# A four-stage transformer step on one core: the last two weight units before each norm walked both in a row for tiles 0 to 2, instead of one tile apart

## The chip, the core and the metric

One core of a Trainium2 chip runs the whole program. The metric is the device time of one execution in microseconds (us). TensorE (PE) multiplies and transposes into PSUM, VectorE (DVE) and ScalarE (ACT) read PSUM and work in SBUF, GpSimd (POOL) works in SBUF only, SyncE (SP) issues loads. They meet through semaphores.

## What is computed

A two-layer decoder trunk over 512 prompt tokens and 64 new tokens (8 sequences of 8). Layer 0 mixes by block-sparse and dilated attention, layer 1 by gated linear attention (GLA). Each layer then has a ConvFFN, and after the mix and after the FFN stands `x <- LayerNorm(alpha*x + f(x))`:

```python
xp = layer_norm(DN_ALPHA * xp + mp, ln_mix_g[l], ln_mix_b[l])       # mp = o @ w_out
fp, cbp = conv_ffn(xp, buf0, ffn_w_up[l], ffn_conv_w[l], ffn_conv_b[l], ffn_w_down[l])
xp = layer_norm(DN_ALPHA * xp + fp, ln_ffn_g[l], ln_ffn_b[l])
```

The same is done for the 64 new tokens. So there are four norms, and in front of each a product with 1024 output columns: stage 0 is the attention output product, stage 1 the down product of layer 0, stage 2 the GLA output product, stage 3 the down product of layer 1. The result of stage 3 is the output.

## The kernel before, in words

Tokens lie in five tiles, 0 to 3 of 128 rows and tile 4 of 64 (`TILES`). Weights come in units of up to 128 x 2048 values. A unit is loaded by SP into one of two `raw` slots, split into a high part by ACT (`split_hi`, L1053) and a low part by DVE (`split_lo`, L1371), and used by PE. A product takes three matmuls per 128 rows of contraction: high by high, high by low, low by high (`three_products`, L614).

A step is one unit by one tile (`project`, L622). Its matmuls of 512 columns go into PSUM bank t for tile t, the same bank for the left and the right half of the output, and it ends with one increment of the semaphore `steps`. A unit of four contraction blocks gives a step of 12 matmuls, one of two blocks a step of 6.

- Stage 0 has two units: the first gives the left half of the output, the second the right half. A step of the second must wait until DVE has read the left half of that tile out of the same bank (`z_read`).
- Stages 1 and 3 have 12 units, six for each half. Units 10 and 11 both add to the right half; unit 11 has two blocks. Its h part, too, has to be split first: high by ACT (`h_split`, L1230), low by DVE (L1576). PE waits for it in `rows_here` (L881).
- Stage 2 has four units, two for each half; units 2 and 3 both add to the right half.

All units but the last two are walked unit by unit, tiles 0 to 4. The last two are walked in the order that the list `PAIR` (L78) gives as (which of the two units, tile). `norm_steps` (L90) puts this order together, and PE (`products_before_norm`, L802) and DVE (`residual_ln`, L1542) both walk it. `norm_sums` (L96) counts the reads of PSUM by it. `freed` (L85) tells after how many steps the first unit of the pair is done with, which is after step (0, 4).

High parts share slots by parity. So ACT can split the second unit of the pair only when the unit before the pair is done with, which is when the first step of the pair begins (stages 1 to 3). It splits the first unit of the next stage when `freed` is reached (`ln_roots`, L1151), after the square root of tile 2. POOL then makes that unit's low part (`split_after_norm`, L1892). PE waits for this low part before it turns the normalised tiles of the next stage.

For each step that completes a half of a tile, DVE adds it to x (L1523, which reads PSUM) and takes the statistics (L1525). When the right half is in, it normalises the tile: L1531, then L1536 `(x - mean) * g`, then L1538 and L1540 `* 1/sd + b`, with ACT's square root (L1155) in between. After tile 3, and before tile 4, DVE makes the low parts of the turned tiles 0 to 2 (L1381) for the next stage.

In stages 0 and 2 PE also turns the convolution's side rows, 44 transposes of 20 columns (`turn_sides`, L796), just ahead of the fifth step from the end of the pair's ten. The side rows are loaded by SP (L526). In stage 0 SP issues these loads, behind the norm's vectors (L518), only when the attention outputs of the samples are ready (`soT_ready`).

Of the kernel before, what the change touches and what calls it, by code (L numbers as in the profile page):

```python
# [74 lines left out]

PAIR = [(0, 0), (0, 1), (1, 0), (0, 2), (1, 1), (0, 3), (1, 2), (0, 4), (1, 3), (1, 4)]  # L78
NORM_UNITS = []
for k_, n_ in (("attn_out", 2), ("down0", 2 * len(DOWN_GROUPS)), ("gla_out", 4), ("down1", 2 * len(DOWN_GROUPS))):  # L80
    NORM_UNITS.append([UNIT_NO[(k_, c_)] for c_ in range(n_)])
# [3 lines left out]
def freed(n):  # L85

    return STEPS_BEFORE[n] + PAIR.index((0, NTILE - 1)) + 1 if n in PAIRED else STEPS_BEFORE[n + 1]


def norm_steps(stage):  # L90

    m = len(NORM_UNITS[stage])
    return [(c, t) for c in range(m - 2) for t in range(NTILE)] + [(m - 2 + a, t) for a, t in PAIR]

# [1943 lines left out]
```

## Time and profile before

| what | value |
|---|---|
| time, median of 3 runs | 1726.14 us (1721.52 to 1729.16) |
| the profiled execution, first to last instruction | 1727.2 us |
| PE busy | 1632.9 us (95%), clock 0.967 on average |
| DVE busy | 911.0 us (53%) |
| ACT busy | 559.0 us (32%) |
| POOL busy | 59.4 us (3%) |

The profiled execution is known by its span alone. It is 1.1 us above the median of the three timed runs and inside their spread. In the rows below, a timeline row has the start, the duration, the engine, the line, the operation, out<-in with shapes, the count, and in brackets how long the engine was idle before and who released it. A duration is the instruction's own; matmuls overlap, so the pace of a row of matmuls is read from their starts. PE idle time "<-issue" is time for which the profile shows no releaser.

### The profile page before, as it was taken

The numbers are of one execution on the slowest core, as the hardware profiler recorded it, in microseconds if no ns is written. First come the engines' busy times: TensorE is split into PE (matmuls) and PEld (weight loads), VectorE is DVE, ScalarE is ACT, GpSimd is POOL, SyncE is SP. The second block draws the span as 40 slices with busy tenths as digits, with TensorE's granted clock in tenths as the row PEclk, the third lists the DMA queues.
The fourth block names the chain that finished last, engine by engine and source line by source line (L and its number), as shares of the span: only waits on it lengthen the run. The fifth ranks groups of instructions, "written<-read, shape, count | busy, mean of one in ns | idle before, by whom it ended". The sixth has DMA issues, their size and how long they took to land.

```text
span 1727.2 us, 24786 instructions
## 1 busy us (share of the span) xinstructions
PE 1632.9 (95%) x9654; PEld 1417.9 (82%) x9654; DVE 911.0 (53%) x1718; ACT 559.0 (32%) x1040; POOL 59.4 (3%) x95
## 2 busy tenths in 40 slices
PE   6999999988899999999989999989989999999996
PEld 5888766656799999988869888866879999998885
DVE  2533243024766666653462276566566666665445
ACT  2212244331334334333222433252133433433321
POOL 1002200000100000000010000010010000000000
PEclk9999999997899999999989899999989999999998
DMA  4223550345132232242131221053113223224211
GB/s 161 95 91 101 191 220 36 109 131 127 49 98 73 73 97 73 73 119 73 62 96 51 67 73 57 25 177 113 49 53 95 73 79 91 73 73 119 74 61 55
DMA packets 150849, 155.82 MB, mean 90 GB/s; under 512 B 7598, under 2 KB 120366, under 8 KB 150542
## 3 DMA queue, kind: packets, MB, share of 16 engines
q1 hardware_dynamic: 146842, 141.70, 26.6%
q0 software_dynamic: 3936, 13.14, 2.4%
q8 instruction: 49, 0.80, 0.2%
q14 instruction: 22, 0.18, 0.0%
HBM read 142.99 MB, written 21.91 MB: 95 GB/s over the span
## 4 chain that ended last, share of the span: by engine, by line
PE 86%; DVE 8%; ACT 4%; issue 2%; DMA 0%; SPq 0%; POOL 0%; DVEq 0%; ACTq 0%; POOLq 0%
PE ps L618 70%; PE ps L599 5%; PE ps L674 2%; PE ps L781 2%; PE ps L945 1%; DVE x_reg L1536 1%; PE ps L978 1%; PE ps L1009 1%; DVE w_lo L1375 1%; ACT w_hi L1059 1%; ACT arena L1091 1%; DVE x_reg L1540 1%; DVE arena L1437 1%; DVE xl_reg L1381 1%; PE ps L708 1%
## 5 line engine op out<-in xcount | busy, mean ns | idle before, releaser
L618 PE MATMUL ps<-xh_reg,w_hi 128*128 128x288 f32 x1552 | 464.5, 299 | 7.5 <-DVE xl_reg L1381 7.5
L618 PE MATMUL ps<-xh_reg,w_lo 128*128 128x288 f32 x1552 | 460.1, 296 | 0.0
L618 PE MATMUL ps<-xl_reg,w_hi 128*128 128x288 f32 x1552 | 460.0, 296 | 0.0
L618 PE MATMUL ps<-w_hi,xh_reg 128*128 128x512 f32 x960 | 385.5, 402 | 6.9 <-DVE xl_reg L1576 3.4
L618 PE MATMUL ps<-w_lo,xh_reg 128*128 128x512 f32 x960 | 378.4, 394 | 0.0
L618 PE MATMUL ps<-w_hi,xl_reg 128*128 128x512 f32 x960 | 378.3, 394 | 0.0
L618 PEld LDWEIGHTS ps<-xh_reg,w_hi 128*128 128x128 f32 x1552 | 294.2, 190 | 9.8 <-DVE xl_reg L1381 5.4
L618 PEld LDWEIGHTS ps<-xl_reg,w_hi 128*128 128x128 f32 x1552 | 294.3, 190 | 0.0
L618 PEld LDWEIGHTS ps<-xh_reg,w_lo 128*128 128x128 f32 x1552 | 294.1, 189 | 0.0
L1375 DVE TENSOR_TENSOR w_lo<-raw,w_hi 128x2048 fp32r<-128x2048 f32 (+1 forms) x52 | 113.8, 2188 | 307.8 <-ACT w_hi L1059 307.8
L618 PEld LDWEIGHTS ps<-w_hi,xh_reg 128*128 128x128 f32 x960 | 183.3, 191 | 47.5 <-issue 7.6
L618 PEld LDWEIGHTS ps<-w_hi,xl_reg 128*128 128x128 f32 x960 | 182.9, 191 | 39.3
L618 PEld LDWEIGHTS ps<-w_lo,xh_reg 128*128 128x128 f32 x960 | 183.3, 191 | 36.2
L1059 ACT ACTIVATE w_hi<-raw 128x2048 fp32r<-128x2048 f32 (+1 forms) x55 | 100.9, 1835 | 259.6 <-PE ps L618 241.0
L1612 DVE SCALAR_TENSOR_TENSOR arena<-arena 128x512 f32<-128x512 f32 x352 | 166.8, 515 | 6.3
L1610 DVE TENSOR_SCALAR arena<-arena 128x512 f32<-128x512 f32 (+1 forms) x176 | 67.7, 427 | 179.3 <-ACT arena L1197 179.3
L1196 ACT ACTIVATE arena<-ps 128x224 f32<-128x224 f32 x88 | 31.5, 358 | 239.5 <-PE ps L618 239.5
L1594 DVE TENSOR_TENSOR w_lo<-raw,w_hi 128x2048 fp32r<-128x2048 f32 x44 | 100.5, 2285 | 3.3 <-ACT w_hi L1183 3.1
L599 PE MATMUL ps<-ident,arena 128*128 128x128 f32 (+3 forms) x434 | 65.6, 284 | 22.5 <-ACT arena L1091 6.3
L599 PEld LDWEIGHTS ps<-ident,arena 128*128 128x128 f32 (+3 forms) x434 | 47.6, 155 | 44.9 <-issue 15.3
L1183 ACT ACTIVATE w_hi<-raw 128x2048 fp32r<-128x2048 f32 x44 | 83.7, 1902 | 0.1
L1194 ACT ACTIVATE arena<-ps 128x288 f32<-128x288 f32 x88 | 36.0, 411 | 112.7 <-PE ps L618 112.7
(168 smaller groups left out, 1450.1 us busy)
## 6 DMA issues: line engine op xcount, KB each, us to landing
raw<-in_ffn_w_up SPq DMA_DIRECT2D x88, 512.0 KB, 5.0
raw<-in_ffn_w_down SPq DMA_DIRECT2D x40, 512.0 KB, 4.6
raw<-in_attn_w_in SPq DMA_DIRECT2D x24, 512.0 KB, 4.9
raw<-in_gla_w_in SPq DMA_DIRECT2D x24, 512.0 KB, 4.4
out_swa_s<-in_state_swa_kv SPq DMA_DIRECT2D x2, 3968.0 KB
x_reg<-in_x_prompt SPq DMA_DIRECT2D x8, 512.0 KB, 5.0
raw<-in_gla_w_out SPq DMA_DIRECT2D x8, 512.0 KB, 4.8
arena<-in_state_swa_kv SPq DMA_DIRECT2D x12, 256.0 KB, 3.3
```

The lines of the kernel that those rows point to most:

```text
L599: last = pe.transpose(ps[0:cols, bank, col:col + rows], src, ident[0:rows, 0:rows])
L618: mm = pe.matmul(out, lhs(i, a), rhs(i, b), start=first and i == 0 and a + b == 0, stop=last and i == ks - 1 and a == 1)
L674: pe.matmul(ps[:, g, 0:(qi + 1) * P - k0], qkT[rows, c, qi * P:(qi + 1) * P], qkT[rows, 8 + c, k0:(qi + 1) * P], start=True, stop=True).th ...
L781: pe.matmul(ps[rows, g, 0:past], qz[:, 2 * g + pair, s].rearrange("p h q -> p (h q)"), kcT[s % 2][:, b:b + past // P, :].rearrange("p b c ...
L1059: act.activation(w_hi[:, n % 2, 0:a], raw[:, n % 2, 0:a], ACT.Copy).then_inc(hi_done, 1)
L1183: act.activation(w_hi[:, slot, :], raw[:, slot, :], ACT.Copy).then_inc(hi_done, 1)
L1194: act.activation(ext[:, u, v, 2:2 + SPLIT], ps[:, m, 0:SPLIT], ACT.Copy).then_inc(ext_ready, 1)
L1196: act.activation(ext[:, u, v, 2 + SPLIT:2 + NP], ps[:, m, 0:PRE], ACT.Copy)
L1375: dve.tensor_tensor(w_lo[:, n % 2, 0:a], raw[:, n % 2, 0:a], w_hi[:, n % 2, 0:a].bitcast(F32), ALU.subtract).then_inc(lo_done, 1)
L1594: dve.tensor_tensor(w_lo[:, slot, :], raw[:, slot, :], w_hi[:, slot, :].bitcast(F32), ALU.subtract).then_inc(lo_done, 1)
L1610: ins = dve.tensor_scalar(y, e, w, fj[:, u, v, SIDE - 1:SIDE], ALU.mult, ALU.add)
L1612: ins = dve.scalar_tensor_tensor(y, e, w, y, ALU.mult, ALU.add)
```

## The change

The order of the ten steps of the pair is another. Nothing else is edited; the functions named above take the order from this list.

```diff
-PAIR = [(0, 0), (0, 1), (1, 0), (0, 2), (1, 1), (0, 3), (1, 2), (0, 4), (1, 3), (1, 4)]
+PAIR = [(0, 0), (1, 0), (0, 1), (1, 1), (0, 2), (1, 2), (0, 3), (0, 4), (1, 3), (1, 4)]
```

The second unit's steps of tiles 0, 1 and 2 are now steps 2, 4 and 6 of the ten (counted from 1), where they were 3, 5 and 7. Step (0, 4) stays the eighth, (1, 3) and (1, 4) stay the last two, so `freed` is the same number. The side rows are still turned ahead of step 6, which is (1, 2) now and was (0, 3).

## Rows read from the trace of the kernel before

**Rows 1.** The page: busy time by engine, and the chain's shares by engine.

```profile
PE 1632.9 (95%) x9654; PEld 1417.9 (82%) x9654; DVE 911.0 (53%) x1718; ACT 559.0 (32%) x1040; POOL 59.4 (3%) x95
...
PE 86%; DVE 8%; ACT 4%; issue 2%; DMA 0%; SPq 0%; POOL 0%; DVEq 0%; ACTq 0%; POOLq 0%
```

**Rows 2.** The chain that ended last: start us, us, what with the count.

```profile
816.98 61.50 PE ps L618 x270
...
1237.85 3.19 PE ps L599 x44
1241.04 13.89 PE ps L618 x48
```

**Rows 3.** Timeline of DVE in the pair of stage 1.

```profile
872.86 1.23 DVE L1375 TENSOR_TENSOR w_lo<-raw,w_hi 128x1024 fp32r<-128x1024 f32 x1 [7.98 <-ACT w_hi L1059]
874.00 1.35 DVE L1576 TENSOR_TENSOR xl_reg<-arena,xh_reg 128x1152 fp32r<-128x1152 f32 x1
878.51 0.69 DVE L1523 SCALAR_TENSOR_TENSOR x_reg<-x_reg,ps 128x512 f32<-128x512 f32 x1 [3.16 <-PE ps L618]
...
882.80 0.68 DVE L1523 SCALAR_TENSOR_TENSOR x_reg<-x_reg,ps 128x512 f32<-128x512 f32 x1
...
891.37 0.68 DVE L1523 SCALAR_TENSOR_TENSOR x_reg<-x_reg,ps 128x512 f32<-128x512 f32 x1
...
893.05 4.04 DVE L1536 SCALAR_TENSOR_TENSOR x_reg<-x_reg,ln_mv,arena 128x1024 f32<-128x1024 f32 x1
```

**Rows 4.** Timelines of ACT and POOL in the pair of stage 1.

```profile
871.76 1.06 ACT L1059 ACTIVATE w_hi<-raw 128x1024 fp32r<-128x1024 f32 x1 [9.67 <-PE ps L618]
...
889.44 1.92 ACT L1059 ACTIVATE w_hi<-raw 128x2048 fp32r<-128x2048 f32 x1 [0.38 <-PE ps L618]
...
891.51 4.50 POOL L1898 TENSOR_TENSOR w_lo<-raw,w_hi 128x2048 fp32r<-128x2048 f32 x1 [134.69 <-ACT w_hi L1059]
```

**Rows 5.** Timelines of DVE and ACT in the pair of stage 0.

```profile
404.80 0.69 DVE L1523 SCALAR_TENSOR_TENSOR x_reg<-x_reg,ps 128x512 f32<-128x512 f32 x1
...
412.41 1.29 DVE L1536 SCALAR_TENSOR_TENSOR x_reg<-x_reg,ln_mv,arena 128x1024 f32<-128x1024 f32 x1 [2.10 <-DMA arena<-in_ln_mix_b]
...
415.00 0.68 DVE L1523 SCALAR_TENSOR_TENSOR x_reg<-x_reg,ps 128x512 f32<-128x512 f32 x1
...
433.64 1.92 ACT L1059 ACTIVATE w_hi<-raw 128x2048 fp32r<-128x2048 f32 x1 [0.79 <-PE ps L618]
```

**Rows 6.** Timeline of PE and SP in the pair of stage 0.

```profile
398.86 0.47 PE L618 MATMUL ps<-w_hi,xh_reg 128*128 128x512 f32 x1
...
405.63 0.47 PE L618 MATMUL ps<-w_hi,xh_reg 128*128 128x512 f32 x1 [1.06 <-DVE x_reg L1523]
...
406.50 0.23 SPq L526 DMA_DIRECT2D arena<-in_ffn_conv_b  x1
...
418.00 4.85 PE L599 MATMUL ps<-ident,arena 20*128 20x20 f32 x44 [3.94 <-issue]
```

**Rows 7.** Busy time by stretch of 2 us: PE, PEld, DVE, ACT, POOL, PEclk, DMA, GB/s.

```profile
404.00:406.00 2.00, 0.94 (x5) 0.50 (x4) 1.89 (x6) 0.00 (x0) 0.00 (x0) 1.00 0.18 55
...
418.00:420.00 2.00, 2.00 (x19) 2.00 (x20) 1.96 (x3) 0.29 (x1) 0.00 (x0) 0.50 0.95 265
...
426.00:428.00 2.00, 2.00 (x7) 1.56 (x6) 0.00 (x0) 0.00 (x0) 0.00 (x0) 0.57 0.00 0
...
1246.00:1248.00 2.00, 2.00 (x9) 1.59 (x8) 0.00 (x0) 0.00 (x0) 0.00 (x0) 0.77 0.00 0
```

**Rows 8.** Timelines of ACT and DVE in the pair of stage 2.

```profile
1224.35 1.92 ACT L1059 ACTIVATE w_hi<-raw 128x2048 fp32r<-128x2048 f32 x1 [11.68 <-PE ps L618]
...
1226.30 2.29 DVE L1375 TENSOR_TENSOR w_lo<-raw,w_hi 128x2048 fp32r<-128x2048 f32 x1 [0.61 <-ACT w_hi L1059]
```

**Rows 9.** Timelines of PE and DVE at the end of stage 3.

```profile
1709.44 0.39 PE L618 MATMUL ps<-w_hi,xl_reg 128*128 128x512 f32 x1
...
1710.49 0.68 DVE L1523 SCALAR_TENSOR_TENSOR x_reg<-x_reg,ps 128x512 f32<-128x512 f32 x1
```

## The prediction

> **What bounds the kernel now.** I began with the page. PE is busy 95% of the span and holds 86% of the chain that ended last, DVE 8% [rows 1]. That is an average; the change touches only four short stretches, so I went on to the chain and to the timelines there.
>
> The chain gives PE's pace: 270 matmuls in 61.50 us are 0.228 us each at the full clock [rows 2]. A step of 12 takes A = 2.73 us, one of 6 takes B = 1.37 us. The 44 side transposes take 3.19 us, and the four steps after them 13.89 us where 4A are 10.9 [rows 2]: 3.0 us go to a lower clock.
>
> The timeline of DVE in stage 1 gives DVE's pace: one tile's residual and norm take 882.80 - 878.51 = 4.29 us [rows 3], more than the A + B = 4.10 us in which PE delivers a tile. DVE is just the slower one there. Tile 3's residual starts at 891.37 [rows 3]. PE had that tile 0.6 us before: its start of the pair is 878.51 less two A, one B and 0.2 us of drain and signal, or 871.5, and tile 3 is complete after 5A + 4B = 19.1 us, so DVE could start at 890.8.
>
> What ends the stage is neither. When step (0, 4) has ended, ACT splits the next unit (889.44, 1.92 us), then POOL makes its low part (891.51, 4.50 us) [rows 4]. DVE's L1536 of tile 3 starts at 893.05 and takes 4.04 us, against 1.28 us for others of its kind; it ends at 897.09, 1.1 us behind POOL's 896.01 [rows 3, 4]. L1523, which ran inside the same POOL instruction and reads PSUM and one tensor of SBUF, kept its 0.68 us [rows 3]. So the end of stages 0 to 2 follows the end of step (0, 4), with 6.6 us of ACT and POOL behind it. The Trainium skill, GPSIMD Engine Reference, Key points, says that POOL shares its SBUF interfaces with VectorE and contends with instructions of two SBUF inputs. By that rule as by these rows the delay of POOL, not that of tile 3's data, counts in stage 1; by tile 3's data alone its term below would be 0.7, not 1.3.
>
> **The change, stage by stage.** No instruction is added or removed: the same steps, reads, DMAs and splits. Moved are PE's steps and DVE's residuals with their norms. Step (0, 4) stays eighth, so what counts is by how much it is late. SP's loads hang on low parts and arrive long before their use; they cost nothing beyond the shifts below.
>
> *Stage 1.* Step (1, 0) is now second and wants unit 11 with its h part one A after the pair's start, at 871.5 + 2.7 = 874.2. They can't come earlier: ACT may start only when unit 9 is done (871.76), then w_lo, then L1576, which ends at 874.00 + 1.35 = 875.35 [rows 3, 4]. With 0.14 us from DVE to PE (405.49 to 405.63 in stage 0 [rows 5, 6]) PE starts at 875.5 and stood 1.3 us. Before, this had 2.7 us more and was hidden. Nothing later gives it back, as PE has no other stall in the pair: step (0, 4), ACT, POOL and L1536 all move by **+1.3 us**. DVE gains 1.5 us on tile 0, which only idles later.
>
> *Stage 0.* Here the wait is for the bank. (1, 0) needs DVE's read of (0, 0), which starts at 404.80 because DVE is busy with the sample outputs till then; PE starts (1, 0) at 405.63 [rows 5, 6]. Before, PE did (0, 0) and (0, 1) first and stood 1.06 us [rows 6]. Now it does (0, 0) from 398.86, stands 4.0 us, and starts (1, 0) at the same 405.63. (0, 1) follows and ends at 411.1. (1, 1) needs the read of (0, 1), and on DVE that is queued behind the norm of tile 0, whose L1536 waits for the norm's vector until 412.41, as before; the next L1523 starts at 415.00 [rows 5]. PE thus starts (1, 1) at 415.8 and has stood 4.7 us. Then come (1, 1) and (0, 2), 5.5 us, until 421.3, and the side transposes. Before, those started at 418.00 after 3.94 us of standing [rows 6]; the view names no releaser, the wait in the code at this place is on the side rows' loads, the last issued at 406.50 [rows 6], so I take that as the cause. Those loads don't move, so 3.94 us of the loss is covered. At the full clock the transposes take 3.2 us instead of 4.85 [rows 2, 6]: until 424.5. Tile 1's norm and the read of (0, 2) end at 418.8 + 4.3 + 0.7 = 423.8, before (1, 2) wants them. The three steps to the end of (0, 4) took 433.6 - 422.85 = 10.8 us [rows 5, 6], with a low clock in it, which I keep: 435.3, or +1.7.
>
> Now the clock. In the 3.94 us of standing the granted clock fell to 0.50, 1.2 GHz, and was back at 2.4 GHz only in the stretch from 426 to 428; the 1.06 us of standing left it at 1.00 [rows 7]. The new 4.7 us is like the former. If it falls, (1, 1) runs at half pace, 5.1 us, all else 2.4 later: +4.1. The Trainium skill, TensorE: Matmul & The Clock Gate, HAM oscillation, says that an idle gap lets the clock fall back to its lower level. By that rule, the trace agrees, one would take the full +4.1. Between the ends 1.7 and 4.1 I take **+3.0 us**: one of the two low stretches is likely, and they may partly fall together. The 4.0 us at 401.6 can also lower the clock, but DVE waits until 412.41 anyway, so (1, 0) and (0, 1) have the 2.10 us of that wait as cover [rows 5].
>
> *Stage 2.* Unit 3: ACT from 1224.35 (1.92 us), DVE from 1226.30 (2.29 us), ready 1228.59 [rows 8], PE at 1228.7. The pair begins at 1224.1, so (1, 0) is wanted at 1226.8: **+2.0 us**, passed on whole, as above. PE waits for no read here, both units add to one half.
>
> *Stage 3.* The same stall of 1.3 us, but no POOL: DVE ends it. PE's last matmul of tile 3 ends at 1709.44 + 0.39 = 1709.83 and DVE takes the tile only at 1710.49 [rows 9]. With PE 1.3 later DVE can start at 1711.2: **+0.7 us**. DVE's early start is lost, since tile 3 now waits for PE.
>
> Sum: 3.0 + 1.3 + 2.0 + 0.7 = +7.0 us. Against the profiled 1727.2 that is 1734.2, against the median of 1726.1 it is **1733.1 us**, +0.41%.
>
> Unknown is only the clock. After the side transposes the low stretch lasted till about 1247 in stage 2 and, with the idle before it, from 418 to 427.7 in stage 0 [rows 7]. One such stretch more or longer is worth 1 to 2.4 us in stages 0 and 2 each, less is possible too.
>
> **Rivals.** *The clock takes more* (chance 0.30). Place: the standing of 4.7 us in stage 0 and the side transposes of stages 0 and 2. At the upper end, stage 0 costs 4.1 and stage 2 costs 2.0 + 2.0, if its low stretch takes as much as 10 us at half pace, 5.0 instead of the 3.0 of rows 2: 10.1 in all, 1736.2 us. It decides from 1.6 us over my sum. For it: the fall after 3.94 us. Against it: the kernel before pays one such stretch too, which may now be shorter.
>
> *Not slower: the early tiles pay* (0.07). DVE is the slower one in stages 1 and 3. If unit 11 were ready when asked, tile 3 would be taken at 890.8 instead of 891.37, -0.6 in stage 3 and 0 in stage 1, where POOL sets the end. In stage 0, if the clock stayed up throughout, (0, 4) would end at 424.5 + 8.2 = 432.7, -0.9. That is -1.5 us, 1724.6. It decides only if the second unit's readiness is less than 2.7 us behind the pair's start; the rows say 4.0 and 4.6. Even if all three POOL collisions went, each as dear as stage 1's 2.8 us, it would be -8.4.
>
> *Partly absorbed* (0.13): the wait of stage 0 is hidden by the side loads and the clock, +0 there, and the rest is +4.0: 1730.1 us.
>
> *Forecast* 0.50. A change of under 0.5%, 8.6 us, is about what a measurement of this kernel can't tell from none. Slower by more: the first rival and a little of the forecast's own spread, 0.32. Faster by more: 0.02, for spread alone, since no mechanism reaches it. Within: 0.66. The range, 1728.0 to 1739.0, takes in the absorbed case, the clock at its dearest with 3 us for the spread of the runs, and leaves out the case that is not slower.
>
> **What would show it.** Right: PE idle ahead of (1, 0), 1.3 us behind L1576 in stages 1 and 3, 2.0 behind L1375 in stage 2, 4.0 behind L1523 in stage 0; 4 to 5 us ahead of (1, 1) in stage 0 and none ahead of the side transposes; the first L1523 of stages 1 and 3 earlier by 1.5 us, that of tile 3 later by 0.7; L1536 of tile 3 still stretched to 1.1 us behind POOL. Wrong: no idle ahead of (1, 0), tile 3's L1536 at 1.28 us, or the stage ends moving by other sums than step (0, 4).

## The result and the profile after

| | before | after |
|---|---|---|
| median | 1725.15 us (1721.52 to 1734.66) | 1730.52 us (1727.5 to 1733.28) |
| executions | 20 | 20 |
| ratio | | 1.0025, 95% interval 1.0016 to 1.0035 |
| span of the profiled execution | 1727.2 us | 1728.3 us |
| mean granted clock in it | 0.967 | 0.973 |

The kernel became slower by 4.3 us (2.8 to 6.0), a quarter of a per cent, under the 0.5% of the forecast. (The medians are 5.4 us apart; I go by the ratio, which has an interval.) The two spans differ by 1.1 us only. Single executions lie up to 13 us apart for the kernel before and 6 us for the changed one. Much of this spread lies ahead of the change: in the twelve profiles of this study the attention part ahead of stage 0 ends anywhere from 393.7 to 404.5 us, whatever was changed behind it. So I compare stretches from anchor to anchor, and not spans.

First the page after, to be held against [rows 1]:

```profile
PE 1626.3 (94%) x9654; PEld 1411.5 (82%) x9654; DVE 912.2 (53%) x1718; ACT 559.1 (32%) x1040; POOL 59.4 (3%) x95
...
PE 86%; DVE 7%; ACT 4%; issue 1%; DMA 1%; SPq 0%; POOL 0%; DVEq 0%; ACTq 0%; POOLq 0%
```

The same instructions, and PE is busy for 6.6 us less than before although the run is longer. Less of its work fell into a low clock. "issue" went from 2% to 1% and DMA from 0% to 1%. Both are small steps made large by rounding: what left the chain is the standing of 3.94 us ahead of the side transposes, 0.2% of the span, and what came is 7.25 us of one load, 0.4%.

PE in the pair of stage 0, from its timeline, against [rows 6]:

```profile
402.90 0.47 PE L618 MATMUL ps<-w_hi,xh_reg 128*128 128x512 f32 x1 [3.79 <-DVE x_reg L1523]
...
413.23 0.47 PE L618 MATMUL ps<-w_hi,xh_reg 128*128 128x512 f32 x1 [2.99 <-DVE x_reg L1523]
...
420.47 2.91 PE L599 MATMUL ps<-ident,arena 20*128 20x20 f32 x44
```

Two waits for a bank: 3.79 us ahead of (1, 0), 2.99 us ahead of (1, 1). Ahead of the transposes there is no bracket, so no idle time. DVE's rows say why (1, 1) waits, against [rows 5]:

```profile
402.07 0.69 DVE L1523 SCALAR_TENSOR_TENSOR x_reg<-x_reg,ps 128x512 f32<-128x512 f32 x1
...
409.80 1.28 DVE L1536 SCALAR_TENSOR_TENSOR x_reg<-x_reg,ln_mv,arena 128x1024 f32<-128x1024 f32 x1 [0.63 <-DMA arena<-in_ln_mix_b]
...
412.40 0.68 DVE L1523 SCALAR_TENSOR_TENSOR x_reg<-x_reg,ps 128x512 f32<-128x512 f32 x1
```

The read of (0, 1), at 412.40, is queued behind tile 0's norm, which waited for the norm's vector until 409.80. The chain that ended last shows this load:

```profile
402.44 7.25 DMA arena<-in_ln_mix_b
```

ACT's splits that follow step (0, 4), in stages 0, 1 and 2, from ACT's timelines, against [rows 5] and [rows 4]:

```profile
433.46 1.92 ACT L1059 ACTIVATE w_hi<-raw 128x2048 fp32r<-128x2048 f32 x1 [3.52 <-PE ps L618]
...
871.64 1.06 ACT L1059 ACTIVATE w_hi<-raw 128x1024 fp32r<-128x1024 f32 x1 [9.67 <-PE ps L618]
...
890.71 1.92 ACT L1059 ACTIVATE w_hi<-raw 128x2048 fp32r<-128x2048 f32 x1 [3.12 <-PE ps L618]
...
1224.86 1.92 ACT L1059 ACTIVATE w_hi<-raw 128x2048 fp32r<-128x2048 f32 x1 [11.68 <-PE ps L618]
...
1253.26 1.92 ACT L1059 ACTIVATE w_hi<-raw 128x2048 fp32r<-128x2048 f32 x1 [3.51 <-PE ps L618]
```

The row at 871.64 marks the start of stage 1's pair, the one at 1224.86 that of stage 2. From these anchors, and the same ones before, the whole comes apart. "Next product" is the 201st matmul of the weight product (L618) after POOL's low part.

| stretch | before, us | after, us | difference |
|---|---|---|---|
| stage 0: start of the pair to the split behind (0, 4) | 34.79 | 37.34 | +2.55 |
| to the next product | 47.75 | 47.81 | +0.06 |
| to the pair of stage 1 | 390.36 | 390.36 | 0.00 |
| stage 1: pair to the split | 17.68 | 19.07 | +1.39 |
| to the next product | 46.91 | 47.84 | +0.93 |
| GLA, to the pair of stage 2 | 288.00 | 286.32 | -1.68 |
| stage 2: pair to the split | 27.95 | 28.39 | +0.44 |
| to the next product | 48.25 | 47.56 | -0.69 |
| to the last pair | 390.34 | 390.36 | +0.02 |
| stage 3: last pair to the end | 36.34 | 37.09 | +0.75 |

The sum is +3.8 us, inside the 2.8 to 6.0 of the timed runs. The stretch of 390 us with no part in the change repeats to 0.02 us, so the differences of half a microsecond and more are real for these two executions. How often another execution would show them is another question, to which the experiments come back.

PE in the pairs of stages 1, 2 and 3, from its timeline:

```profile
875.37 0.47 PE L618 MATMUL ps<-w_hi,xh_reg 128*128 128x512 f32 x1 [1.11 <-DVE xl_reg L1576]
...
1229.16 0.50 PE L618 MATMUL ps<-w_hi,xh_reg 128*128 128x512 f32 x1 [1.67 <-DVE w_lo L1375]
...
1694.91 0.47 PE L618 MATMUL ps<-w_hi,xh_reg 128*128 128x512 f32 x1 [1.11 <-DVE xl_reg L1576]
```

Each stall stands where it was expected, behind the instruction that was named. The brackets are some 0.2 us short of the delays, since a matmul's 0.39 or 0.47 us reaches past the 0.228 us in which the next could have followed. Tile 3 of stage 1, on DVE and POOL, against [rows 3] and [rows 4]:

```profile
877.03 0.69 DVE L1523 SCALAR_TENSOR_TENSOR x_reg<-x_reg,ps 128x512 f32<-128x512 f32 x1 [1.81 <-PE ps L618]
...
892.01 0.69 DVE L1523 SCALAR_TENSOR_TENSOR x_reg<-x_reg,ps 128x512 f32<-128x512 f32 x1 [2.04 <-PE ps L618]
...
893.71 4.66 DVE L1536 SCALAR_TENSOR_TENSOR x_reg<-x_reg,ln_mv,arena 128x1024 f32<-128x1024 f32 x1
```

```profile
892.78 4.51 POOL L1898 TENSOR_TENSOR w_lo<-raw,w_hi 128x2048 fp32r<-128x2048 f32 x1 [136.09 <-ACT w_hi L1059]
```

Tile 0 is taken 1.4 us earlier against the pair's start (5.39 us behind 871.64, before 6.75 behind 871.76), and DVE makes nothing of it: it then idles 2.04 us ahead of tile 3. L1536 of tile 3 ends at 898.37, 1.1 us behind POOL's 897.29.

Last the clock, in the windows of 2 us (columns as in [rows 7], PEclk third from the end):

```profile
414.00:416.00 2.00, 2.00 (x6) 1.61 (x5) 0.00 (x0) 0.00 (x0) 0.00 (x0) 0.50 0.96 242
...
420.00:422.00 2.00, 2.00 (x28) 1.65 (x26) 1.96 (x3) 0.00 (x0) 0.00 (x0) 1.00 0.06 18
422.00:424.00 2.00, 2.00 (x26) 1.88 (x25) 1.51 (x3) 1.07 (x2) 0.00 (x0) 1.00 0.00 0
424.00:426.00 2.00, 2.00 (x7) 1.57 (x6) 0.00 (x0) 0.00 (x0) 0.00 (x0) 0.55 0.00 0
...
1128.00:1130.00 2.00, 1.84 (x9) 1.64 (x10) 1.76 (x3) 1.97 (x3) 0.00 (x0) 1.00 1.03 351
...
1244.00:1246.00 2.00, 2.00 (x6) 1.52 (x5) 0.00 (x0) 0.00 (x0) 0.00 (x0) 0.50 0.00 0
1246.00:1248.00 2.00, 2.00 (x8) 1.60 (x7) 0.24 (x1) 0.00 (x0) 0.00 (x0) 0.79 0.00 0
```

In stage 0 the clock fell behind either bank wait and once more behind the transposes, each time to 0.50 (1.2 GHz) for 3.4 us. Before it was one stretch of about 10 us [rows 7]. In stage 2 the stretch behind the transposes is 3.4 us long, before 6.8.

The GLA part gives 1.7 us back in two places, and a third, where one looks first, gives nothing. Before and after, in this order:

```profile
970.00:972.00 2.00, 1.99 (x6) 1.25 (x5) 0.00 (x0) 1.15 (x3) 0.00 (x0) 0.61 0.18 69
970.00:972.00 2.00, 1.68 (x7) 1.37 (x8) 0.00 (x0) 0.61 (x3) 0.00 (x0) 1.00 1.00 375
```

```profile
1134.12 0.70 PE L993 MATMUL ps<-arena 128*128 128x256 f32 x2 [1.13 <-DVE arena L1770]
1135.13 0.70 PE L993 MATMUL ps<-arena 128*128 128x256 f32 x2 [2.82 <-DVE arena L1770]
```

The first place is a low stretch that lasted from 970.4 to 980.7 us before and lasts from 973.8 to 980.6 after: PE comes to it 2.2 us late and is 1.0 us late some 40 us on. The second is the low stretch from 1188.9 to 1195.7, which stands at the same time in both: PE comes to it 1.0 us late, less of its work falls in, and it is 0.5 us late behind it. Between them the profile before has a low stretch from 1127.4 to 1130.9 and the one after has none. PE does the work there 1.7 us faster after, but then waits for DVE 2.82 us instead of 1.13, and is 1.01 us late on either side. A low stretch costs nothing where another engine sets the pace.

### The profile page after: what moved, and what is told of

Same layout as the page of the kernel before. It is cut to its first block, busy times and chain, and to the rows that moved or that the text cites. A ratio compares the mean times of both kernels' runs of the same rounds, so it can differ in the third digit from the quotient of the medians.

```text
span 1728.3 us, 24786 instructions
## 1 busy us (share of the span) xinstructions
PE 1626.3 (94%) x9654; PEld 1411.5 (82%) x9654; DVE 912.2 (53%) x1718; ACT 559.1 (32%) x1040; POOL 59.4 (3%) x95
## 4 chain that ended last, share of the span: by engine, by line
PE 86%; DVE 7%; ACT 4%; issue 1%; DMA 1%; SPq 0%; POOL 0%; DVEq 0%; ACTq 0%; POOLq 0%
PE ps L618 71%; PE ps L599 5%; PE ps L674 2%; PE ps L781 2%; PE ps L945 1%; DVE w_lo L1375 1%; ACT w_hi L1059 1%; PE ps L978 1%; PE ps L1009 1%; DVE x_reg L1536 1%; ACT arena L1091 1%; DVE arena L1437 1%; DVE xl_reg L1381 1%; PE ps L708 1%; PE ps L865 1%
## 5 line engine op out<-in xcount | busy, mean ns | idle before, releaser
L618 PE MATMUL ps<-xh_reg,w_hi 128*128 128x288 f32 x1552 | 464.8, 299 | 7.5 <-DVE xl_reg L1381 7.5
L618 PE MATMUL ps<-xh_reg,w_lo 128*128 128x288 f32 x1552 | 460.3, 297 | 0.0
L618 PE MATMUL ps<-xl_reg,w_hi 128*128 128x288 f32 x1552 | 460.3, 297 | 0.0
L618 PE MATMUL ps<-w_hi,xh_reg 128*128 128x512 f32 x960 | 385.7, 402 | 16.5 <-DVE x_reg L1523 8.3
L618 PE MATMUL ps<-w_lo,xh_reg 128*128 128x512 f32 x960 | 378.7, 395 | 0.0
L618 PE MATMUL ps<-w_hi,xl_reg 128*128 128x512 f32 x960 | 378.3, 394 | 0.0
L618 PEld LDWEIGHTS ps<-xh_reg,w_hi 128*128 128x128 f32 x1552 | 294.4, 190 | 9.8 <-DVE xl_reg L1381 5.4
L618 PEld LDWEIGHTS ps<-xl_reg,w_hi 128*128 128x128 f32 x1552 | 294.7, 190 | 0.0
L618 PEld LDWEIGHTS ps<-xh_reg,w_lo 128*128 128x128 f32 x1552 | 294.4, 190 | 0.0
L618 PEld LDWEIGHTS ps<-w_hi,xh_reg 128*128 128x128 f32 x960 | 183.1, 191 | 58.6 <-issue 16.7
L618 PEld LDWEIGHTS ps<-w_hi,xl_reg 128*128 128x128 f32 x960 | 183.1, 191 | 39.5
L618 PEld LDWEIGHTS ps<-w_lo,xh_reg 128*128 128x128 f32 x960 | 183.2, 191 | 36.1
L1059 ACT ACTIVATE w_hi<-raw 128x2048 fp32r<-128x2048 f32 (+1 forms) x55 | 100.9, 1835 | 267.1 <-PE ps L618 250.5
L599 PE MATMUL ps<-ident,arena 128*128 128x128 f32 (+3 forms) x434 | 62.7, 275 | 18.1 <-ACT arena L1091 6.3
L599 PEld LDWEIGHTS ps<-ident,arena 128*128 128x128 f32 (+3 forms) x434 | 44.9, 144 | 40.6 <-issue 10.9
```

Of the source, the lines that this page charges most:

```text
L599: last = pe.transpose(ps[0:cols, bank, col:col + rows], src, ident[0:rows, 0:rows])
L618: mm = pe.matmul(out, lhs(i, a), rhs(i, b), start=first and i == 0 and a + b == 0, stop=last and i == ks - 1 and a == 1)
L1059: act.activation(w_hi[:, n % 2, 0:a], raw[:, n % 2, 0:a], ACT.Copy).then_inc(hi_done, 1)
```

## The experiments

Ten kernels ran, each 6 to 12 times beside the kernel before on the same chip. All of them compute the whole step. Each was profiled once, so what a profile shows is shown for one execution.

### One stage at a time

The list becomes one per stage, with the new order in some stages and the old in the others. In these three kernels lines behind the list are 3 higher than in the profile (L621 for L618).

```diff
-PAIR = [(0, 0), (1, 0), (0, 1), (1, 1), (0, 2), (1, 2), (0, 3), (0, 4), (1, 3), (1, 4)]
+PAIRS = [[(0, 0), (1, 0), (0, 1), (1, 1), (0, 2), (1, 2), (0, 3), (0, 4), (1, 3), (1, 4)],
+         [(0, 0), (0, 1), (1, 0), (0, 2), (1, 1), (0, 3), (1, 2), (0, 4), (1, 3), (1, 4)],
+         [(0, 0), (0, 1), (1, 0), (0, 2), (1, 1), (0, 3), (1, 2), (0, 4), (1, 3), (1, 4)],
+         [(0, 0), (0, 1), (1, 0), (0, 2), (1, 1), (0, 3), (1, 2), (0, 4), (1, 3), (1, 4)]]
...
-    return [(c, t) for c in range(m - 2) for t in range(NTILE)] + [(m - 2 + a, t) for a, t in PAIR]
+    return [(c, t) for c in range(m - 2) for t in range(NTILE)] + [(m - 2 + a, t) for a, t in PAIRS[stage]]
```

This is s0_only, as a diff to the changed kernel. s13_only has the new order in the second and fourth list, s2_only in the third; `freed` takes its stage's list.

> The new order in stage 0 alone. Theory (each stage pays its own stall, the sum is what the change costs): +2.5 to +3 us against the kernel before, since step (0, 4) ended 2.6 us later after the pair's start in the profile of the changed kernel (37.3 against 34.8 us). Rival A (the bank wait of stage 0 is the whole cost): +4.3 us, all of what was measured. Rival B (stage 0's standing is covered by the side rows' loads): 0. In the profile all expect PE idle for about 3.8 us ahead of (1, 0) and 3 to 5 us ahead of (1, 1), and stages 1 to 3 as before.

Measured: ratio 1.0021 (1.0009 to 1.0033), +3.6 us (1.6 to 5.7). This stage alone makes a difference that the timing sees. It excludes 0 and can't tell the theory's 2.5 to 3 us from rival A's 4.3. PE in its pair, from the timeline:

```profile
411.28 0.76 PE L621 MATMUL ps<-w_hi,xh_reg 128*128 128x512 f32 x1 [3.79 <-DVE x_reg L1526]
421.77 0.47 PE L621 MATMUL ps<-w_hi,xh_reg 128*128 128x512 f32 x1 [2.41 <-DVE x_reg L1526]
429.05 2.91 PE L602 MATMUL ps<-ident,arena 20*128 20x20 f32 x44
```

Both stalls are there, the second 0.6 us shorter than in the full change. The split behind (0, 4) came after 35.93 us, 1.1 us later than before, where the full change had +2.55: here no low stretch follows the transposes. In this execution the bank waits, with the low stretches right behind them, are worth 1.1 us; a low stretch behind the transposes, which may come or not, is worth some 1.4 us more. The rest of the +3.6 us isn't in stage 0 in this profile: the GLA part, in which nothing was changed, took 291.19 us for 288.00, and behind stage 2's split 1.9 us came back.

> The new order in stages 1 and 3 alone, where unit 11 is not ready one step after the pair's start. Theory: +1.4 in stage 1 and +0.7 in stage 3, +2.1 us together, with the POOL split of stage 1 starting 1.4 us later after the pair's start. Rival A (stage 0 is the whole cost): 0. Rival C (DVE's early start on tiles 0 to 2 pays in the stages where it is the slower engine): -0.6 us or less.

Measured: ratio 0.9995 (0.9981 to 1.0008), -0.9 us (-3.3 to +1.4). My terms for stages 1 and 3 were +1.3 and +0.7 us, together 1.0012, and that lies outside the interval. By its number this is rival A, but not by its reason, for the stalls are there: pair to split 19.08 us in stage 1, last pair to the end 37.12, just as in the full change. What takes their cost away is behind them: the GLA stretch is 286.37 us (before 288.00), and stage 2's pair, in the old order, takes 24.85 us where it took 27.95. PE's transposes of stage 2, and the clock behind them:

```profile
1233.34 2.91 PE L602 MATMUL ps<-ident,arena 20*128 20x20 f32 x44
```

```profile
1236.00:1238.00 2.00, 2.00 (x12) 1.66 (x12) 1.78 (x3) 0.54 (x1) 0.00 (x0) 1.00 0.00 0
1238.00:1240.00 2.00, 2.00 (x11) 1.64 (x10) 0.00 (x0) 0.00 (x0) 0.00 (x0) 1.00 0.00 0
```

Before, the clock stood at 0.50 for 6.8 us from the end of these transposes on (1240.1 to 1246.9). Here the same steps in the same order stay at 1.00.

> The new order in stage 2 alone, where the low part of unit 3 is not ready. The standing of PE is 1.8 us in every case. Theory by the prediction's sum: +2.0 us. Rival D (most of it is given back, because the low clock after the side transposes is met for a shorter time, as in the profile of the changed kernel, where step (0, 4) ended only 0.4 us later): +0.4 us; then the low stretch after the side transposes is 3.4 us here too and not 6.8. Rival A: 0.

Measured: ratio 1.0001 (0.9985 to 1.0017), +0.2 us (-2.6 to +2.9). The timing alone can't tell 0 from my +2.0. The profile can: PE stood 1.68 us ahead of (1, 0), and the pair took 28.43 us to the split, 0.48 more than before. The low stretch behind the transposes was 3.4 us as in the full change, and this is what rival D expected. Against s13_only, whose stage 2 met no low stretch, the full change's 28.39 us is 3.54 longer: the stall of 1.8 and one low stretch of 3.4 us at half pace, 1.7.

### The same delay made of work

If the stall is not special, PE work of equal length at the same place must do the same. The kernel before, with extra matmuls into an unused bank just ahead of step (1, 0) of stage 1, which is there the third of the pair:

```diff
+                    if stage == 1 and (c, t) == (11, 0):
+                        for i in range(6):
+                            pe.matmul(ps[:, 7, :], xTh[:, 0, 0:P], of_unit(w_hi, n, kn)[:, 0, :], start=i == 0, stop=i == 5)
                     project(n, t, k0, kn, g == 0, g == len(groups(0)) - 1)
```

This is pad6; pad12 has twelve. Nothing reads what they give.

> The kernel before with six more matmuls of 512 columns into an unused bank ahead of step (1, 0) of stage 1, 1.4 us of pure work for PE, the size of the stall that the new order gives stage 1. Theory (a delay of this size in stage 1 is given back later by the clock, as in s13_only, where PE spent less time at 1.2 GHz): step (0, 4) of stage 1 ends 1.4 us later after the pair's start, but the time is 2 to 3 us shorter than before, with a shorter low stretch at the start of the GLA part and after the side transposes of stage 2. Rival (s13_only came out low for another reason, DVE's early start or chance): +1.4 us, and the low stretches as before.

Measured: ratio 0.9992 (0.9975 to 1.0008), -1.4 us (-4.3 to +1.4). The chain of waits shows the work that was added on it:

```profile
871.67 1.36 PE ps L819 x6
```

Stage 1's pair took 19.04 us to the split, 1.36 more. Then the profile does what s13_only's did: GLA 286.36 us, stage 2's pair 24.85. From stage 1's pair to the next product of stage 2 the two agree stretch by stretch within 0.05 us. So in these profiles neither stall nor order makes the gain, only the delay of about 1.4 us. The timing supports less: +1.4, what plain adding up gives, is the very end of the interval, and the 2 to 3 us of gain that I expected are inside it but not shown. The next twelve:

> The same with twelve matmuls, 2.7 us of pure work. Rival (work simply adds up): +2.7 us. Theory: not proportional to the delay; the stall is 2.7 us, and what the clock gives back is again about 1.7 us or a multiple of it, so between -2 and +3 us, with the low stretches elsewhere than in pad6.

Measured: ratio 1.0003 (0.9991 to 1.0015), +0.5 us (-1.6 to +2.6). The added work is 12 times 0.228 or 2.73 us, 1.0016, just outside the interval. Pair to split 20.40 us (+2.72), next product +0.34, GLA +0.12, stage 2's pair -1.60, behind it -0.82: +0.8 in all. Twice the delay gives back as well, at other places. It is no fixed refund of 1.4 us, but a question of which low stretches the delayed work meets.

### The bank wait taken away

The new order in all stages, but in stage 0 the right halves of tiles 0 to 2 go to banks that are free: (1, 0) to 4, (1, 1) to 0, (1, 2) to 1. Each step waits for the read of the step that had its bank last; the matmuls and DVE's read take the bank from `bank_of`. Lines behind are 11 to 14 higher (L629 for L618, L610 for L599, L1073 for L1059).

```diff
+def bank_of(stage, c, t):
+    return {(1, 0): 4, (1, 1): 0, (1, 2): 1}.get((c, t), t) if stage == 0 else t
+HELD = {(1, 1): (0, 0), (1, 2): (0, 1), (0, 4): (1, 0), (1, 3): (0, 3), (1, 4): (0, 4)}
...
-                    if half == 1 and g == 0:
+                    if stage == 0:
+                        if (c, t) in HELD:
+                            pe.wait_ge(z_read, sums.index(HELD[(c, t)]) + 1)
+                    elif half == 1 and g == 0:
```

> The changed kernel, but in stage 0 the right half goes to another bank: (1, 0) to bank 4, (1, 1) to bank 0, (1, 2) to bank 1, each free by then, so that no step waits for DVE's read of the left half of the same tile. Nothing else. Theory (the bank wait is what costs in stage 0): PE doesn't stand ahead of (1, 0) nor ahead of (1, 1), reaches the side transposes about 5 steps of 2.73 us after the pair's start and stands there for the side rows' loads instead, as the kernel before did; (0, 4) ends 34.8 us after the pair's start, 2.6 us less than in the changed kernel, so +1.7 us against the kernel before instead of +4.3. Rival (DVE, not the bank, sets stage 0): the same time as the changed kernel, +4.3 us.

Measured: ratio 1.0013 (1.0000 to 1.0026), +2.2 us (0.0 to 4.5); the full change has +4.3 (2.8 to 6.0). The intervals overlap, so the difference is likely and not proven by the timing. The profile has it: start to split 34.38 us, 2.96 less than the full change and 0.4 less than before. PE and ACT in stage 0, from their timelines:

```profile
414.69 4.85 PE L610 MATMUL ps<-ident,arena 20*128 20x20 f32 x44 [4.98 <-issue]
```

```profile
430.06 1.92 ACT L1073 ACTIVATE w_hi<-raw 128x2048 fp32r<-128x2048 f32 x1 [3.55 <-PE ps L629]
```

No bank stall is left, and in its place PE stands 4.98 us ahead of the transposes, which again run at the low clock, 4.85 us. They begin 19.0 us behind the start of the pair, before 19.1, though PE was there sooner. So two things compete for the same time in stage 0, the bank waits and the wait at the side rows, and whoever comes first covers the other. That the second is for the loads is read from the code (`side_loaded`) and from the time: the transposes begin 11.4 us behind the last issue of these loads here and 11.5 before. The profile shows no landing for them, so it isn't shown directly.

### The split released one step earlier

If the end of step (0, 4) sets the stage's end, move (0, 4) forward. Stages 0 to 2 take this order, stage 3 the old one:

```diff
+[(0, 0), (0, 1), (1, 0), (0, 2), (0, 3), (1, 1), (0, 4), (1, 2), (1, 3), (1, 4)]
```

> The order of the pair in stages 0 to 2 is (0,0) (0,1) (1,0) (0,2) (0,3) (1,1) (0,4) (1,2) (1,3) (1,4): the first unit is done with after seven steps, one sooner than in either kernel; stage 3 as before. Theory (the end of stages 0 to 2 follows the end of step (0, 4) by way of ACT and POOL): POOL's split starts one step sooner, 2.7 us in stages 0 and 2 and 1.4 in stage 1, and the time is 2 to 6 us shorter. Rival (tile 3's own chain on DVE ends the stage): no change or slower by up to 2 us, with L1536 of tile 3 at 1.3 us.

Measured: ratio 1.0038 (1.0024 to 1.0053), +6.6 us (4.1 to 9.1). A clear miss. ACT's timeline in stage 0 shows what I had not counted:

```profile
434.06 0.29 ACT L1158 ACTIVATE ln_sd<-ln_mv,eps_ln 128x1 f32<-128x1 f32 x1 [4.44 <-DVE ln_mv L1534]
434.26 1.90 ACT L1062 ACTIVATE w_hi<-raw 128x2048 fp32r<-128x2048 f32 x1
```

The split stands behind tile 2's square root in ACT's queue, and waits for nothing of its own: it has no bracket. The order makes tile 2 complete after (0, 4), so that tile's statistics and root set the release. Pair to split is 36.67 us in stage 0, 19.72 in stage 1 and 29.79 in stage 2, against 34.79, 17.68 and 27.95 before. Step (0, 4) decides only as long as tile 2's root is earlier. The theory as put is refuted: the end of (0, 4) alone doesn't set the release.

### The side rows turned last

The wait at the side rows and the low clock behind it are there before the change too. In the next kernel the 44 transposes go ahead of the last step of the pair instead of ahead of the fifth from the end, and ACT's copy of them from behind tile 1's root to behind tile 3's. The order of steps is the old one.

```diff
-                    if stage % 2 == 0 and (c, t) == norm_steps(stage)[-5]:
+                    if stage % 2 == 0 and (c, t) == norm_steps(stage)[-1]:
...
-                    if stage % 2 == 0 and t == 1:
-                        take_sides()
...
+                    if t == 3 and stage % 2 == 0:
+                        take_sides()
```

> The kernel before with its old order, but the side rows of stages 0 and 2 are turned ahead of the last of the ten steps instead of ahead of the sixth, and ACT takes them after the square root of tile 3. Theory (in stage 0 PE's standing of 3.94 us is the side rows' loads, and the end of a stage follows step (0, 4)): (0, 4) of stage 0 ends about 11 us sooner, the side transposes start without standing, and the time is 8 to 12 us shorter, to about 1715. Rival (the side rows are needed before the stage can end anyway, or the standing had another cause): within 3 us of the kernel before, with PE standing somewhere else.

Measured: ratio 0.9902 (0.9882 to 0.9922), median 1709.3 us, 16.9 us less than before (13.5 to 20.4). It beats both kernels, and by more than I had expected. PE, ACT and POOL in its stage 0, and last the row of the kernel before that answers to PE's third:

```profile
411.11 0.47 PE L618 MATMUL ps<-w_hi,xh_reg 128*128 128x512 f32 x1 [1.05 <-DVE x_reg L1523]
430.32 2.91 PE L599 MATMUL ps<-ident,arena 20*128 20x20 f32 x44
...
437.62 1.03 PE L599 MATMUL ps<-ident,x_reg 128*128 128x128 f32 x8
```

```profile
429.05 1.90 ACT L1059 ACTIVATE w_hi<-raw 128x2048 fp32r<-128x2048 f32 x1
```

```profile
431.12 4.80 POOL L1898 TENSOR_TENSOR w_lo<-raw,w_hi 128x2048 fp32r<-128x2048 f32 x1 [222.46 <-ACT w_hi L1059]
```

```profile
440.37 1.09 PE L599 MATMUL ps<-ident,x_reg 128*128 128x128 f32 x8 [1.37 <-POOL w_lo L1898]
```

Start to split is 24.72 us instead of 34.79. Step (0, 4) ends 11.3 us sooner, as expected: the standing of 3.94 and the transposes of 4.85 us [rows 6] no longer lie ahead of it, that is 8.8, and the other 2.5 are the low clock behind them. The split gains only 10.1 of this. It has no bracket, as in free_early: it now waits 1.3 us for tile 2's root (428.85). The transposes run beside ACT's split and POOL's low part. The tail to the next product is 3.3 us shorter as well (44.47 for 47.75). PE comes to the turned tiles 8.6 us behind the split, before 6.7, now without the 1.37 us of standing for POOL. What it gains is behind that: before, the clock was at 0.50 from 444.8 to 455.0 us, which costs 5.1 us at half pace, here it is at 1.00 from 436.6 on. That tail is what my expectation lacked. Stage 2 gives 6.2 and 4.4 us in the same two stretches. The GLA part was 3.0 longer in this execution, and the two long products 0.6 and 1.0, for which I have no cause. From the start of stage 0's pair to the end this profile is 19.7 us shorter than the one before.

> The changed kernel, and the side rows turned ahead of the last step as in sides_old. Theory (in stage 0 the side rows' loads and the transposes behind them cover part of the new order's standing, the prediction's 3.94 us): without this cover the new order costs more than the 4.3 us measured. By the rows of the kernel before, (1, 2) of stage 0 now waits for DVE too, and (0, 4) ends about 33 us after the pair's start, 8 us later than in sides_old; with +1.4, +1.8 and +0.7 in stages 1 to 3 that is 10 to 13 us over sides_old, or 4 to 7 us under the kernel before. Rival (no cover; the new order costs what it cost): 4.3 us over sides_old, 12.6 us under the kernel before.

The same edit with the new order in all four stages. Measured: ratio 0.9975 (0.9959 to 0.9991), 1720.94 us. It lies 11.6 us above sides_old (medians 1720.94 and 1709.3; the kernel before had the same 1726.24 beside both). Start to split in stage 0 is 34.84 us, 10.1 more than in sides_old. PE's timeline there:

```profile
403.17 0.47 PE L621 MATMUL ps<-w_hi,xh_reg 128*128 128x512 f32 x1 [3.77 <-DVE x_reg L1526]
413.25 0.47 PE L621 MATMUL ps<-w_hi,xh_reg 128*128 128x512 f32 x1 [2.74 <-DVE x_reg L1526]
422.69 0.47 PE L621 MATMUL ps<-w_hi,xh_reg 128*128 128x512 f32 x1 [2.12 <-DVE x_reg L1526]
```

Without the transposes as a cover, (1, 2) waits for its bank as well. Step (0, 4) ends 11.4 us later than in sides_old, where I expected 8. The stalls are 8.6 us of it, less the 1.05 that the old order stands, and the two low stretches behind them (404.4 to 407.8 and 414.6 to 418.0) up to 3.4; those I hadn't counted. The split is only 10.1 later, since in sides_old it waits for the root. This is the price of the new order when nothing hides it, and the rival's 4.3 us is excluded.

> sides_new with the right halves of tiles 0 to 2 of stage 0 in other banks, as in banks. Theory (the standing in stage 0 is the wait for the bank): (0, 4) of stage 0 ends as in sides_old again or is held by tile 2's norm on DVE, within 1 us, and the time is 2 to 5 us over sides_old, 12 to 15 under the kernel before. Rival (DVE's queue sets stage 0 in this order whatever the bank): the same as sides_new.

New order, side rows last, and the spread banks. Measured: ratio 0.9938 (0.9915 to 0.9960), 1715.51 us, 6.2 above sides_old and 10.7 (6.9 to 14.7) under the kernel before, a little worse than expected. Start to split is 25.16 us, close to the old order's 24.72. But the waits for DVE's reads aren't gone, as PE's timeline shows:

```profile
410.74 0.47 PE L629 MATMUL ps<-w_hi,xh_reg 128*128 128x512 f32 x1 [2.66 <-DVE x_reg L1537]
...
421.94 0.47 PE L629 MATMUL ps<-w_hi,xh_reg 128*128 128x512 f32 x1 [2.78 <-DVE x_reg L1537]
```

The first is step (1, 2), which takes bank 1 after the left half of tile 1. This bank is not free by then: its read is queued behind the norm of tile 0. The second is (1, 3), which needs the read of (0, 3). It stands behind (0, 4), so the split doesn't see it, but the tail does: behind it the clock falls twice, and the tail is 49.08 us for 44.47. Over both stretches, from the start of the pair to the next product, stage 0 takes 69.2 us in sides_old, 78.7 in sides_new and 74.2 in sides_banks. So the new order costs 9.5 us there, and other banks save 4.4 of them; what is left goes with these two waits and the low clock behind the second. In the timing it is 11.6 and 6.2 us over sides_old. The new order's stalls in the other stages stay: +1.4 in stage 1, +2.0 in stage 2 (23.73 against 21.76) and +0.8 in stage 3; GLA is 2.2 shorter. These are single profiles.

## Why the prediction was right, and where it was not

The forecast was 1733.1 us, measured were 1730.52. In the increment that is +7.0 against +4.3 (2.8 to 6.0). The stalls stand where they were foretold, so the mechanism was right; of the four terms two hold in size, and two were largely given back behind the stall.

**Stage 0, predicted +3.0, measured +2.6.** Step by step, as times from the pair's start: (1, 1) was to begin at 16.9 us and began at 17.1; the transposes were to begin at 22.4 and began at 24.35; the split was to come at 37.8 and came at 37.34. The 1.9 us in the middle are mostly the low clock behind the wait for (1, 1), for which I had put 2.4 as the dearest case. About 1.0 us came back at the transposes and after: these ran in 2.91 us where I took 3.2, and the three steps behind them took 10.1 us where I kept 10.8. So 1.7 plus 1.9 less 1.0 make the 2.6. That my +3.0 is close is partly luck: it was a middle between two ends, taken for one low stretch of two, and both came. One sign missed: ahead of (1, 1) PE stood 2.99 us and not 4 to 5, since (1, 0) and (0, 1) had run 1.7 us slower in the low stretch before it. Right were both covers: no idle ahead of the transposes, and in banks, where the bank waits are gone, PE stands there again; and the low stretch behind the first wait (403.7 to 407.1) cost only DVE's wait for the norm's vector, 0.63 us where it was 2.10 [rows 5].

**Stage 1, predicted +1.3, measured +1.4 at the split but only +0.6 in all.** The stall, its length and its releaser were right, and so was what sets the stage's end: L1536 ended 1.1 us behind POOL, as before. That instruction took 4.66 us in stage 1 and 3.37 in stages 0 and 2, others of its kind 1.28. The Trainium skill, GPSIMD Engine Reference, Key points, says that POOL contends with VectorE's instructions of two SBUF inputs; the trace agrees. The tail then took 0.9 us more, and the GLA part gave 1.7 back, where one low stretch was 3.4 us shorter and less work fell into another. "Nothing later gives it back" held for the pair and not for what follows.

**Stage 2, predicted +2.0, measured -0.2.** This is the term that failed, in its words "passed on whole". PE stood nearly as computed, 1.8 us for 2.0, but the low stretch behind the transposes halved, from 6.8 to 3.4 us, and gave 1.7 back. I had kept the clock as in the profile before and named the clock as an unknown that takes more or, at best, "less is possible too". s13_only and pad6 show it from the other side: a delay of 1.4 us, of a stall or of plain work, makes the whole low stretch vanish, and 3.1 us of the pair with it.

**Stage 3, predicted +0.7, measured +0.75.** Tile 3's read came later by that much; nothing stands behind it that could give anything back.

**The rivals.** "The clock takes more" did not happen: the mean granted clock over all twenty executions was 0.972, over 35 executions of the kernel before 0.969, and PE's busy time went down. Yet it stays possible for single executions, since s0_only and after differ by one low stretch of 1.4 us in the same pair. "Partly absorbed" with its 1730.1 us is the nearest number, but by its place it is wrong: stage 0 was not absorbed (+2.6), stages 1 and 2 were. "Not slower" is excluded by the interval. The first L1523 of stages 1 and 3 was 1.4 us earlier, nobody used it.

What is open: why a low stretch ends sooner or does not come. The runs suggest that the time at which the work arrives matters: two kernels with the same delay in stage 1, one by stalls and one by work, have the same stretches behind it (s13_only and pad6, within 0.05 us). It isn't all, for s0_only, not delayed in stage 1 and 2, has a GLA part 3.2 us longer than before. They don't show by which rule, and single profiles of each kernel can't say how often each course is taken. The sum of the parts does not equal the whole either: +3.6, -0.9 and +0.2 against +4.3, with intervals of 4 to 5 us each.

## What to carry to other kernels

Where an order alternates between two steps that share a PSUM bank, the distance between them is the cover for the read and for everything that stands ahead of the read in VectorE's queue; count both before bringing them together. Before moving the steps, look at what stands between them and the release of the next stage: here moving 44 small transposes behind that release gave 16.9 us, more than any order of the steps changed. Spreading the banks helps only as far as the other bank has been read by then. And a delay of one or two microseconds in a stretch where the clock moves can't be added up by itself; time the whole, and compare profiles stretch by stretch between anchors.

## What the runs showed of the hardware that was not expected

- Added work that takes no time. Six matmuls, 1.36 us on the critical chain, gave a ratio of 0.9992 (0.9975 to 1.0008); behind their delay the GLA part was 1.6 us shorter, with a shorter low stretch at its start, and the low stretch in stage 2 was gone (27.95 to 24.85 us).
- A low stretch can be free. The one from 1127.4 to 1130.9 us in the profile before made PE 1.7 us slower, and PE only stood 1.13 us instead of 2.82 for DVE behind it.
- The granted clock fell without an idle gap directly ahead. PE was busy from 413.23 on in the profile after, the last 2.9 us with transposes of 20 columns, and at 424 the clock went to 0.50 for 3.4 us. The same transposes were followed by none in stage 0 of s0_only and in stage 2 of s13_only and pad6. The Trainium skill, TensorE: Matmul & The Clock Gate, HAM oscillation, tells of idle gaps as what lowers the clock; the falls at 403.7 and 414.0, behind 3.79 and 2.99 us of standing, agree, the fall at 424 shows that it isn't the only way. Without this fall the split of stage 0 would have come up to 1.7 us earlier, an estimate from half pace for 3.4 us.
- How well the courses repeat. With the side rows in their old place the GLA stretch took one of two lengths: 286.32 to 286.37 us in the four profiles where stage 1 was late by 1.4 us (after, s13_only, banks, pad6), and 287.94 to 288.12 us in four of the five others, where it was late by 0, 2.0 or 2.7 us (before, s2_only, free_early, pad12; s0_only, late by 0 too, had 291.19). The long products took 390.3 to 390.4 us in all nine.
- Of the stretched L1536 the end is fixed, not the duration. In stage 0 of sides_old it began 3.3 us into POOL's instruction and took 2.59 us, in stage 1 of the changed kernel it began 0.9 us into it and took 4.66; both times, and in the 3.37 us of stage 0 after the change too, it ended 1.1 us behind POOL. POOL's instruction took 4.80 us there and 4.51 here.
